# A hybrid decoder trunk on one core: one wait ahead of a table load, a weight split amid the squares, a head's sum one block later

## The chip, the cores and the metric

The kernel runs on one core of a Trainium2 chip. Times are device microseconds of one execution; the time before is the median of 3 runs.

## The reference

The reference is a trunk of two layers over 256 tokens of width 1024, batch 1, all in float32. Each layer adds to the residual stream x half of a SwiGLU block of the normed x, then a mixer, then half of another SwiGLU block:

```python
def swiglu(h, w_in, w_out):
    gate, up = jnp.split(h @ w_in, 2, axis=-1)
    return (jax.nn.silu(gate) * up) @ w_out

for i in range(DEPTH):                       # DEPTH = 2, N_A = 1
    x = x + 0.5 * swiglu(rms_norm(x, ffn1_norm[i]), ffn1_w_in[i], ffn1_w_out[i])
    hm = rms_norm(x, mix_norm[i])
    x = x + (retention(hm, ...) if i < N_A else window_attention(hm, k_sh, v_sh, ...))
    x = x + 0.5 * swiglu(rms_norm(x, ffn2_norm[i]), ffn2_w_in[i], ffn2_w_out[i])
    if i == N_A - 1:
        k_sh, v_sh = shared_kv(x, kv_norm, kv_w, k_norm)
```

The inner width of SwiGLU is 2816. Retention has 4 heads of key width 256 and value width 512, with a decay mask; its result is normed for each head, `out * rsqrt(mean(out * out) + eps) * silu(g)`, and multiplied by a matrix of 2048 x 1024. The attention of the second layer has 16 query heads, 2 key heads and a window of 128.

## The kernel before

**Numbers in two parts.** The products run on TensorE in the type fp32r. A weight tile and an activation tile are each split into a high part (`w_hi`, `h` columns 0 to 255), which ScalarE copies out, and a low part (`w_lo`, columns 256 to 511), which VectorE gets by subtraction. A block of 128 x 128 weights then takes two matmuls: high weights times both parts of the activations (512 columns), low weights times the high part (256 columns). The two halves of the result are added in the evacuation: ScalarE copies the low half out of PSUM (L365, L398), VectorE adds it to the high half (L712, L758).

**Units and slots.** All weights are laid out as 1 MB units of 2048 columns (units of the output products are somewhat smaller) and pass through four slots of `stage`, `w_hi` and `w_lo`. SyncE loads unit u when the low part of unit u - 4 is done (`lo_ready`), ScalarE's `split` (L323) waits for `landed` and, from unit 4 on, for `used`; VectorE's `split` (L641) waits for `hi_ready`; TensorE waits for `lo_ready` and increments `used`. Each engine has its own instruction stream, written out by hand in order; semaphores tie them together.

**The start.** Units 0 and 1 are loaded as eight quarters and unit 2 as two halves; ahead of each quarter a tile of x is loaded (x tile 1 and the gains from ScalarE's queue, L607 and L608, all else from SyncE's). For each of the eight tiles ScalarE makes the high part of h (L344: x times the norm's gain) and of the quarter (L613), VectorE the low parts (L687, L1090). TensorE has 9 warm-up matmuls ahead (L1581). The factor 1/rms of a token isn't needed for the products; it is applied in the evacuation (L718). So the squares of x come behind the splits of units 0 to 2: ScalarE makes four activations of two tiles each (L621), VectorE adds them up (`first_sums`, L1069), then unit 3 is split on both engines. TensorE sums over the partitions with a matmul by ones (`norm_sum`, L1177). For the first norm this stands in group 1 behind the four blocks of kt 4, which is the first quarter of unit 3, and it waits for `in_free` 3 (L1244), since it writes to a bank of group 0, and for `sum_added`. VectorE's `first_groups` (L732) begins with `add_halves_of(0)` (L712), which increments `in_free`.

**The retention's end.** GpSimd sums the squares of a head's output (L1141, L1145), TensorE sums over partitions (`head_sum`, L1356), VectorE makes the root (`norm_y`, L939), ScalarE stores the high part of y (L499) and VectorE the low part (L959, `y_lo`). The output projection has 8 tiles (d) of 16 blocks (k); the first 12 blocks of a tile need heads 0 to 2 alone. While the last head is being normed, TensorE does `early[d]` blocks of tiles 0 to 3: 12, 12, 12 and 4. The last head's sum stands behind the blocks of tile 0 (L1378). Then it waits for `y_lo` and does the other blocks, tile by tile.

Of the kernel before, what the change touches and what calls it, by code (L numbers as in the profile page):

```python
# [23 lines left out]
ALU = mybir.AluOpType  # L24
# [16 lines left out]
HEADS_R, DK, DV = 4, 256, 512  # L41
# [81 lines left out]
def trunk(nc, x_t, gains, w_in, w_out, w_ret, w_ret_out, w_kv, w_q, w_o, rot, decay, rope, head_gains,  # L123
# [29 lines left out]
    x_sq = at("x_sq", [P, DT, T], F32, aux + 8192)  # L153
# [33 lines left out]
    gain = at("gain", [P, (NORMS + 1) * DT], F32, misc + 25600)  # L187
# [10 lines left out]
    sem = nc.alloc_semaphore  # L198
# [3 lines left out]
    x_loaded = [sem(f"x_loaded{d}") for d in range(DT)]  # L202
    first_landed = [sem(f"first_landed{d}") for d in range(DT)]
    first_hi, first_lo = sem("first_hi"), sem("first_lo")
    half_landed, half_hi, half_lo = sem("half_landed"), sem("half_hi"), sem("half_lo")
    gains_loaded, rot_loaded = sem("gains_loaded"), sem("rot_loaded")
    rope_loaded, mask_loaded = sem("rope_loaded"), sem("mask_loaded")
    ones_ready, tables_ready = sem("ones_ready"), sem("tables_ready")
    x_squared = sem("x_squared")
# [56 lines left out]
    with nc.Block() as block:  # L266
# [55 lines left out]
        def _(act):  # L322
            def split(u, i=0):  # L323

                n, s = columns(u), u % SLOTS
                if not n:
                    return
                if u >= SLOTS:

                    act.wait_ge(used, u - SLOTS + 1 + 4 * i)  # L330

                act.wait_ge(landed[s], 16 * (u // SLOTS + 1) + 16 * i)
                nc.scalar.activation(w_hi[:, s, 0:n], stage[:, s, 0:n], ACT.Copy).then_inc(hi_ready, 1)  # L333

            def h_hi_tile(m, d, i=0, per=0):

                if m:

                    act.wait_ge(x_done, CREDIT + DT * (m - 1) + d + 1 + per * i)
                else:  # L340
                    act.wait_ge(x_loaded[d], 16)

                act.wait_ge(gains_loaded, 16)
                nc.scalar.activation(h[:, ds(d + per * i, 1), 0:T], x[:, ds(d + per * i, 1), :], ACT.Copy,  # L344
                                     scale=gain[:, ds(m * DT + d + per * i, 1)]).then_inc(h_hi, 1)

# [257 lines left out]
                    if d in (4, 7):  # L604
                        split(v + {4: 2, 7: 3}[d])

            act.dma_start(gain[:], gains).then_inc(gains_loaded, 16)  # L607
            act.dma_start(x[:, 1, :], x_t[1, :, :]).then_inc(x_loaded[1], 16)  # L608
            for d in range(DT):
                s, cols = quarter(d)  # L610
# [4 lines left out]
            for q in range(2):  # L615
# [2 lines left out]
                nc.scalar.activation(w_hi[:, 2, cols], stage[:, 2, cols], ACT.Copy).then_inc(  # L618
                    hi_ready if q else half_hi, 1)
            for k in range(4):  # L620
                nc.scalar.activation(x_sq[:, 2 * k:2 * k + 2, :], x[:, 2 * k:2 * k + 2, :],  # L621
                                     ACT.Square).then_inc(x_squared, 1)
            split(3)
            ffn(0)
            for c in range(HEADS_R):
                ret_head(c)
# [11 lines left out]
        def _(dve):  # L638
            chain = Chain(dve, dve_chain)

            def split(u, i=0, per=4):  # L641

                n, s = columns(u), u % SLOTS
                if not n:
                    return

                dve.wait_ge(hi_ready, u + 1 + per * i)
                nc.vector.tensor_tensor(w_lo[:, s, 0:n], stage[:, s, 0:n], w_hi[:, s, 0:n].bitcast(F32),  # L648
                                        ALU.subtract).then_inc(lo_ready, 1)
# [418 lines left out]

            def first_sums():  # L1069

                dve.wait_ge(x_squared, 4)
                half = x_sq[:, 0:4, :]
                chain.step(nc.vector.tensor_tensor(half, half, x_sq[:, 4:8, :], ALU.add))
                chain.step(nc.vector.tensor_tensor(x_sq[:, 0:2, :], x_sq[:, 0:2, :], x_sq[:, 2:4, :], ALU.add))
                nc.vector.tensor_tensor(sq_sum[:], x_sq[:, 0, :], x_sq[:, 1, :], ALU.add).then_inc(sum_added, DT)

            dve.sem_inc(in_free, CREDIT)
# [21 lines left out]
                nc.vector.tensor_tensor(w_lo[:, 2, cols], stage[:, 2, cols], w_hi[:, 2, cols].bitcast(F32),  # L1099
                                        ALU.subtract).then_inc(lo_ready if q else half_lo, 1)  # L1100
            first_sums()
            split(3)
            ffn(0)
            retention()
            ffn(1)
# [47 lines left out]
        def _(pe):  # L1153
# [202 lines left out]
            def head_sum(c):  # L1356


                pe.wait_ge(sum_added, added_for(RET) + c)
                pe.wait_ge(sum_read, sums_before(RET) + c)  # L1360
                matmul(ps[:, SUM, 0:T], ones[:], sq_sum[:], True, True).then_inc(sum_done, 1)

            def retention():
                with pe.Fori(0, 2) as i:
                    ret_head(0, i)
                    ret_head(1, i)
                u0 = FIRST["ret_out", 0]
                three = YT - YT // HEADS_R
                early = (three, three, three, 4, 0, 0, 0, 0)

                pe.wait_ge(pair_free, 4 + 4 * HEADS_R)
                pe.wait_ge(y_lo, HEADS_R - 1)
                for d in range(4):
                    pe.wait_ge(lo_ready, u0 + d + 1)
                    for k in range(early[d]):
                        weight_block(d, (u0 + d) % SLOTS, k, y_t[:, k, :], k == 0, False)
                    if d == 0:
                        head_sum(HEADS_R)  # L1378

                pe.wait_ge(y_lo, HEADS_R)  # L1380
                for d in range(DT):
                    if d >= 4:
                        pe.wait_ge(lo_ready, u0 + d + 1)
                    for k in range(early[d], YT):
                        last = weight_block(d, (u0 + d) % SLOTS, k, y_t[:, k, :], k == 0, k == YT - 1)
                    last.then_inc(used, 1)
# [272 lines left out]
```

## Time and profile before

| what | us |
|---|---|
| time, median of 3 runs | 1018.96 |
| lowest and highest run | 1018.81, 1019.04 |
| the profiled execution's own time | 1018.74 |
| its span (first to last instruction) | 1016.9 |
| TensorE busy | 1012.0 |
| VectorE busy | 779.8 |
| ScalarE busy | 496.9 |
| GpSimd busy | 95.8 |

The profile has one execution. Engines: PE is TensorE's matmuls, PEld its weight loads, DVE is VectorE, ACT is ScalarE, POOL is GpSimd, SP is SyncE; a name with q (ACTq, SPq) is that engine's queue of waits and DMA issues. L344 is line 344 of the kernel before. Matmuls overlap, so what counts of them is the distance from start to start. "idle before <- releaser" is how long an engine stood idle before a row and what ended it. The granted TensorE clock is full in every slice of the span.

### The profile page before, as it was taken

Reading aid. Unit: us, or ns where it says so; the run is one execution under the profiler, and the core shown is the slowest. Engines: PE = TensorE matmul, PEld = TensorE weight load, DVE = VectorE, ACT = ScalarE, POOL = GpSimd, SP = SyncE. Lnnn points to the kernel's source line nnn. Section 1 sums busy time; section 2 is a strip of 40 time slices with the busy share of each in tenths; the row PEclk is TensorE's granted clock in tenths of the full one; section 3 lists DMA queues with packets and bytes.
Section 4 is the critical chain, followed back from the end, with each engine's and each line's share of the span. In section 5 each row is a group of like instructions: output and inputs, shape, how many; then the busy total and the mean of one; then the engine's idle time right before and its main releaser. Section 6 shows DMA issues by size and latency. Waiting matters only on the chain.

```text
span 1016.9 us, 15833 instructions
## 1 busy us (share of the span) xinstructions
PE 1012.0 (100%) x5922; PEld 885.1 (87%) x5922; DVE 779.8 (77%) x874; ACT 496.9 (49%) x536; POOL 95.8 (9%) x91
## 2 busy tenths in 40 slices
PE   9999999999999999999999999999999999999998
PEld 8888888888888888888888888888887898888888
DVE  7988867788788687777767787787778977877743
ACT  7455445544444364455444454465447944554432
POOL 0000013101100151000014100000210041000000
PEclk9999999999999999999999999999999999999999
DMA  9664456652553454555455645545563345544461
GB/s 345 243 239 174 142 176 220 248 207 103 204 189 117 172 184 153 206 201 167 147 185 203 248 165 189 192 145 171 183 240 120 105 161 192 207 165 167 154 195 63
DMA packets 32295, 185.31 MB, mean 182 GB/s; under 512 B 3840, under 2 KB 6400, under 8 KB 16128
## 3 DMA queue, kind: packets, MB, share of 16 engines
q1 hardware_dynamic: 31968, 184.64, 51.3%
q8 instruction: 23, 0.38, 0.1%
q10 hardware_dynamic: 288, 0.16, 0.1%
q14 instruction: 16, 0.13, 0.0%
HBM read 183.73 MB, written 1.05 MB: 182 GB/s over the span
## 4 chain that ended last, share of the span: by engine, by line
PE 98%; ACT 0%; POOL 0%; DMA 0%; issue 0%; DVE 0%; POOLq 0%; ACTq 0%
PE ps L1155 98%; PE ps L1455 1%; DMA gain<-gains_dram 0%; POOL y_sq L1141 0%; PE ps L1422 0%; ACT w_hi L333 0%; ACT L344 0%; ACT y_sq L493 0%; POOL sq_sum L1145 0%; ACT gate L471 0%; ACT h L344 0%; DVE h L687 0%; PE ps L1414 0%; DVE x L813 0%; POOLq L1138 0%
## 5 line engine op out<-in xcount | busy, mean ns | idle before, releaser
L1155 PE MATMUL ps<-h,w_hi 128*128 128x512 f32 x1664 | 581.3, 395 | 0.4 <-DVE h L687 0.4
L1155 PE MATMUL ps<-h,w_lo 128*128 128x256 f32 x1664 | 462.2, 278 | 0.0
L648 DVE TENSOR_TENSOR w_lo<-stage,w_hi 128x2048 fp32r<-128x2048 f32 (+1 forms) x190 | 397.2, 2099 | 27.5 <-ACT w_hi L333 27.2
L1155 PEld LDWEIGHTS ps<-h,w_hi 128*128 128x128 f32 x1664 | 311.8, 187 | 72.2 <-issue 0.5
L333 ACT ACTIVATE w_hi<-stage 128x2048 fp32r<-128x2048 f32 (+1 forms) x190 | 326.9, 1728 | 6.6 <-PE ps L1155 6.2
L1155 PEld LDWEIGHTS ps<-h,w_lo 128*128 128x128 f32 x1664 | 313.0, 188 | 0.5
L1155 PE MATMUL ps<-act_t,w_hi 128*128 128x512 f32 (+1 forms) x726 | 244.8, 386 | 0.0
L1155 PE MATMUL ps<-act_t,w_lo 128*128 128x256 f32 x704 | 195.8, 278 | 0.0
L1155 PEld LDWEIGHTS ps<-act_t,w_hi 128*128 128x128 f32 x726 | 134.7, 188 | 29.3
L365 ACT ACTIVATE tmp<-ps 128x1024 f32<-128x1024 f32 x44 | 45.1, 1025 | 194.2 <-PE ps L1155 194.2
L1155 PEld LDWEIGHTS ps<-act_t,w_lo 128*128 128x128 f32 x704 | 132.5, 188 | 0.0
L712 DVE TENSOR_TENSOR tmp<-ps,tmp 128x1024 f32<-128x1024 f32 x44 | 53.8, 1223 | 70.0 <-ACT tmp L365 70.0
L398 ACT ACTIVATE tmp<-ps 128x256 f32<-128x256 f32 x39 | 14.9, 381 | 120.0 <-PE ps L1155 120.0
L1155 PE MATMUL ps<-w_hi,h 128*128 128x512 f32 x192 | 59.8, 393 | 0.0
L758 DVE SCALAR_TENSOR_TENSOR tmp<-ps,tmp 128x256 f32<-128x256 f32 x39 | 16.5, 422 | 54.1 <-ACT tmp L398 54.0
L370 ACT ACTIVATE tmp<-tmp 128x512 f32<-128x512 f32 x44 | 27.9, 633 | 59.1 <-DVE tmp L718 59.1
L718 DVE TENSOR_TENSOR tmp<-tmp,r_row 128x1024 f32<-128x1024 f32 x44 | 53.9, 1225 | 1.5
L1127 POOL TENSOR_TENSOR sq_sum<-sq_sum,sq 128x256 f32<-128x256 f32 x35 | 48.4, 1384 | 2.7
L1155 PE MATMUL ps<-y_t,w_hi 128*128 128x512 f32 x128 | 45.3, 399 | 0.0
L1118 POOL TENSOR_TENSOR sq_sum<-x 128x256 f32<-128x256 f32 x5 | 3.1, 615 | 443.6 <-DVE x L760 380.5
L1124 POOL TENSOR_TENSOR sq<-x 128x256 f32 x35 | 31.0, 885 | 130.8 <-DVE x L760 128.8
L1155 PEld LDWEIGHTS ps<-w_hi,h 128*128 128x128 f32 x192 | 35.4, 188 | 8.0 <-issue 0.7
(158 smaller groups left out, 737.6 us busy)
## 6 DMA issues: line engine op xcount, KB each, us to landing
stage<-w_in_dram SPq DMA_DIRECT2D x85, 1024.0 KB, 4.8
stage<-w_out_dram SPq DMA_DIRECT2D x64, 704.0 KB, 4.1
stage<-w_ret_dram SPq DMA_DIRECT2D x24, 1024.0 KB, 4.8
stage<-w_ret_out_dram SPq DMA_DIRECT2D x8, 1024.0 KB, 4.8
stage<-w_q_dram SPq DMA_DIRECT2D x4, 1024.0 KB, 5.3
stage<-w_o_dram SPq DMA_DIRECT2D x4, 1024.0 KB, 4.8
stage<-w_in_dram SPq DMA_DIRECT2D x8, 256.0 KB, 4.2
stage<-w_in_dram SPq DMA_DIRECT2D x2, 512.0 KB, 6.3
```

Source lines behind the costliest of these rows:

```text
L333: nc.scalar.activation(w_hi[:, s, 0:n], stage[:, s, 0:n], ACT.Copy).then_inc(hi_ready, 1)
L365: nc.scalar.activation(t, ps[:, 4 * (g % 2):4 * (g % 2) + 4, T:2 * T], ACT.Copy).then_inc(in_lo_half, 1)
L370: nc.scalar.activation(tmp[:, g % 2, 0:512], tmp[:, g % 2, 0:512], ACT.Silu).then_inc(in_silu, 1)
L398: nc.scalar.activation(tmp[:, d % 2, 0:T], ps[:, bank, T:2 * T], ACT.Copy, scale=scale).then_inc(out_lo_half, 1)
L648: nc.vector.tensor_tensor(w_lo[:, s, 0:n], stage[:, s, 0:n], w_hi[:, s, 0:n].bitcast(F32), ALU.subtract).then_inc(lo_ready, 1)
L712: nc.vector.tensor_tensor(t, ps[:, 4 * (g % 2):4 * (g % 2) + 4, 0:T], t, ALU.add).then_inc(in_free, 1)
L718: nc.vector.tensor_tensor(t, t, same(r_row[:], 4), ALU.mult).then_inc(in_scaled, 1)
L758: chain.step(nc.vector.scalar_tensor_tensor(t, ps[:, bank, 0:T], scale, t, ALU.mult, ALU.add))
L1124: nc.gpsimd.tensor_tensor(sq[:].rearrange("p (a n) -> p a n", a=1), x[:, ds(i + 1, 1), :], x[:, ds(i + 1, 1), :], ALU.mult).then_inc(sq_do ...
L1127: nc.gpsimd.tensor_tensor(sq_sum[:], sq_sum[:], sq[:], ALU.add).then_inc(sum_added, 1)
L1155: return nc.tensor.matmul(out_, w, x_, start=start, stop=stop)
L1455: last = nc.tensor.transpose(ps[:, P_T_BANKS[e][r], q * P:(q + 1) * P], s[:, h0 + head, kb * P:(kb + 1) * P], ident[:])
```

## The change

- The semaphore `gains_loaded` is gone. The gains' load increments `x_loaded[0]`, for which tile 0 now waits at 32 instead of 16; the second wait ahead of every h tile's activation on ScalarE (L343) is gone.
- ScalarE splits unit 3 behind the second of its four activations of squares instead of behind the fourth.
- VectorE adds the first two pairs (512 columns), splits unit 3, and then adds the other two pairs (512), both sums (512) and the two halves (256); before, it added 1024, 512 and 256 columns and then split unit 3.
- TensorE takes the last head's sum behind block 0 of tile 1 instead of behind block 11 of tile 0, and does 6 instead of 4 blocks of tile 3 ahead of the wait for `y_lo`.

```diff
--- before.py
+++ after.py
@@ -203,7 +203,7 @@
     first_landed = [sem(f"first_landed{d}") for d in range(DT)]
     first_hi, first_lo = sem("first_hi"), sem("first_lo")
     half_landed, half_hi, half_lo = sem("half_landed"), sem("half_hi"), sem("half_lo")
-    gains_loaded, rot_loaded = sem("gains_loaded"), sem("rot_loaded")
+    rot_loaded = sem("rot_loaded")
     rope_loaded, mask_loaded = sem("rope_loaded"), sem("mask_loaded")
     ones_ready, tables_ready = sem("ones_ready"), sem("tables_ready")
     x_squared = sem("x_squared")
@@ -338,9 +338,7 @@
 
                     act.wait_ge(x_done, CREDIT + DT * (m - 1) + d + 1 + per * i)
                 else:
-                    act.wait_ge(x_loaded[d], 16)
-
-                act.wait_ge(gains_loaded, 16)
+                    act.wait_ge(x_loaded[d], 16 if d else 32)
                 nc.scalar.activation(h[:, ds(d + per * i, 1), 0:T], x[:, ds(d + per * i, 1), :], ACT.Copy,
                                      scale=gain[:, ds(m * DT + d + per * i, 1)]).then_inc(h_hi, 1)
 
@@ -604,7 +602,7 @@
                     if d in (4, 7):
                         split(v + {4: 2, 7: 3}[d])
 
-            act.dma_start(gain[:], gains).then_inc(gains_loaded, 16)
+            act.dma_start(gain[:], gains).then_inc(x_loaded[0], 16)
             act.dma_start(x[:, 1, :], x_t[1, :, :]).then_inc(x_loaded[1], 16)
             for d in range(DT):
                 s, cols = quarter(d)
@@ -618,9 +616,10 @@
                 nc.scalar.activation(w_hi[:, 2, cols], stage[:, 2, cols], ACT.Copy).then_inc(
                     hi_ready if q else half_hi, 1)
             for k in range(4):
+                if k == 2:
+                    split(3)
                 nc.scalar.activation(x_sq[:, 2 * k:2 * k + 2, :], x[:, 2 * k:2 * k + 2, :],
                                      ACT.Square).then_inc(x_squared, 1)
-            split(3)
             ffn(0)
             for c in range(HEADS_R):
                 ret_head(c)
@@ -1068,10 +1067,12 @@
 
             def first_sums():
 
+                dve.wait_ge(x_squared, 2)
+                chain.step(nc.vector.tensor_tensor(x_sq[:, 0:2, :], x_sq[:, 0:2, :], x_sq[:, 2:4, :], ALU.add))
+                split(3)
                 dve.wait_ge(x_squared, 4)
-                half = x_sq[:, 0:4, :]
-                chain.step(nc.vector.tensor_tensor(half, half, x_sq[:, 4:8, :], ALU.add))
-                chain.step(nc.vector.tensor_tensor(x_sq[:, 0:2, :], x_sq[:, 0:2, :], x_sq[:, 2:4, :], ALU.add))
+                chain.step(nc.vector.tensor_tensor(x_sq[:, 4:6, :], x_sq[:, 4:6, :], x_sq[:, 6:8, :], ALU.add))
+                chain.step(nc.vector.tensor_tensor(x_sq[:, 0:2, :], x_sq[:, 0:2, :], x_sq[:, 4:6, :], ALU.add))
                 nc.vector.tensor_tensor(sq_sum[:], x_sq[:, 0, :], x_sq[:, 1, :], ALU.add).then_inc(sum_added, DT)
 
             dve.sem_inc(in_free, CREDIT)
@@ -1099,7 +1100,6 @@
                 nc.vector.tensor_tensor(w_lo[:, 2, cols], stage[:, 2, cols], w_hi[:, 2, cols].bitcast(F32),
                                         ALU.subtract).then_inc(lo_ready if q else half_lo, 1)
             first_sums()
-            split(3)
             ffn(0)
             retention()
             ffn(1)
@@ -1366,7 +1366,7 @@
                     ret_head(1, i)
                 u0 = FIRST["ret_out", 0]
                 three = YT - YT // HEADS_R
-                early = (three, three, three, 4, 0, 0, 0, 0)
+                early = (three, three, three, 6, 0, 0, 0, 0)
 
                 pe.wait_ge(pair_free, 4 + 4 * HEADS_R)
                 pe.wait_ge(y_lo, HEADS_R - 1)
@@ -1374,8 +1374,8 @@
                     pe.wait_ge(lo_ready, u0 + d + 1)
                     for k in range(early[d]):
                         weight_block(d, (u0 + d) % SLOTS, k, y_t[:, k, :], k == 0, False)
-                    if d == 0:
-                        head_sum(HEADS_R)
+                        if (d, k) == (1, 0):
+                            head_sum(HEADS_R)
 
                 pe.wait_ge(y_lo, HEADS_R)
                 for d in range(DT):
```

## Rows read from the trace of the kernel before

**Rows 1.** The page's busy table of the engines (share of the span).

```profile
PE 1012.0 (100%) x5922; PEld 885.1 (87%) x5922; DVE 779.8 (77%) x874; ACT 496.9 (49%) x536; POOL 95.8 (9%) x91
```

**Rows 2.** The chain of waits of the whole span: start us, us, what.

```profile
345.01 415.12 PE ps L1155 x2402
```

**Rows 3.** Timeline of the start: start us, us, engine, line, what, idle before.

```profile
1.19 0.45 ACTq L608 DMA_DIRECT2D x<-x_t_dram  x1
...
1.53 3.90 PE L1155 MATMUL ps<-ones 128*128 128x128 f32 x18 [1.53 <-DVE ones L1082]
...
3.34 1.28 ACT L344 ACT_TABLE_LOAD   x1 [3.34 <-DMA gain<-gains_dram]
...
4.63 0.51 ACT L344 ACTIVATE h<-x,gain 128x256 fp32r<-128x256 f32 x1
...
5.05 0.61 ACT L613 ACTIVATE w_hi<-stage 128x512 fp32r<-128x512 f32 x1
...
5.80 1.16 PE L1155 MATMUL ps<-h,w_hi 128*128 128x512 f32 x4 [0.37 <-DVE h L687]
```

**Rows 4.** Timeline of ScalarE around its other early table load.

```profile
32.10 1.28 ACT L370 ACT_TABLE_LOAD   x1
34.51 0.63 ACT L370 ACTIVATE tmp<-tmp 128x512 f32<-128x512 f32 x1 [1.13 <-DVE tmp L718]
```

**Rows 5.** DMA issues at 0.74, 1.19 and 8.78: KB, us to landing.

```profile
x<-x_t_dram SPq DMA_DIRECT2D x1, 128.0 KB, 2.3
gain<-gains_dram ACTq DMA_DIRECT2D x1, 28.0 KB, 2.5
...
stage<-w_in_dram SPq DMA_DIRECT2D x1, 256.0 KB, 3.2
...
stage<-w_in_dram SPq DMA_DIRECT2D x1, 1024.0 KB, 8.7
```

**Rows 6.** Timeline of ScalarE between unit 2 and the first copy.

```profile
15.99 2.17 ACT L621 ACTIVATE x_sq<-x 128x512 f32<-128x512 f32 x4
18.07 1.90 ACT L333 ACTIVATE w_hi<-stage 128x2048 fp32r<-128x2048 f32 x1
```

**Rows 7.** Timeline of VectorE in the same stretch.

```profile
14.84 2.51 DVE L1099 TENSOR_TENSOR w_lo<-stage,w_hi 128x1024 fp32r<-128x1024 f32 x2 [1.38 <-ACT w_hi L618]
...
19.46 0.69 DVE L1074 TENSOR_TENSOR x_sq<-x_sq 128x512 f32<-128x512 f32 x1
20.27 0.43 DVE L1075 TENSOR_TENSOR sq_sum<-x_sq 128x256 f32<-128x256 f32 x1
20.61 2.29 DVE L648 TENSOR_TENSOR w_lo<-stage,w_hi 128x2048 fp32r<-128x2048 f32 x1
22.81 1.22 DVE L712 TENSOR_TENSOR tmp<-ps,tmp 128x1024 f32<-128x1024 f32 x1
```

**Rows 8.** Waits between 14 and 30 us, then TensorE's timeline there.

```profile
PEld ps L1155 <- DVE w_lo L648: 0.3, 1, 0.3
...
24.47 0.59 PE L1155 MATMUL ps<-sq_sum,ones 128*128 128x256 f32 x2
...
25.13 0.28 PE L1155 MATMUL ps<-h,w_lo 128*128 128x256 f32 x1
```

**Rows 9.** Timeline of GpSimd and TensorE at the last head's sum.

```profile
344.22 0.74 POOL L1145 TENSOR_TENSOR sq_sum<-y_sq 128x256 f32<-128x256 f32 x1 [0.16 <-POOL y_sq L1141]
...
345.01 0.30 PEld L1155 LDWEIGHTS ps<-sq_sum,ones 128*128 128x128 f32 x2 [0.40 <-POOL sq_sum L1145]
...
345.77 0.28 PE L1155 MATMUL ps<-y_t,w_lo 128*128 128x256 f32 x1
```

**Rows 10.** Timeline of VectorE and TensorE at the output projection's start.

```profile
353.89 1.22 DVE L959 TENSOR_TENSOR y_t<-y_f,y_t 128x1024 fp32r<-128x1024 f32 x1 [1.20 <-ACT y_t L499]
...
355.26 0.41 PE L1155 MATMUL ps<-y_t,w_hi 128*128 128x512 f32 x1
...
358.84 2.29 DVE L648 TENSOR_TENSOR w_lo<-stage,w_hi 128x2048 fp32r<-128x2048 f32 x1 [3.72 <-ACT w_hi L333]
```

## The prediction

> **What bounds the kernel now.** I read the busy table first, then the chain of waits, then the timelines of the two stretches that the diff touches. The busy table gives TensorE 1012.0 us of a span of 1016.9 [rows 1]. The chain leaves TensorE for more than 0.1 us at two places before the tail only: the start, and the sum of the last retention head, from which a single piece of TensorE work of 415.12 us runs on [rows 2]. So an edit counts only as far as it moves a moment at which TensorE stands still; work on ScalarE or VectorE counts only through such a wait. The profiled execution took 1018.74 us, 1.84 us more than its span and 0.22 us less than the median of 1018.96; I sum changes in its trace and add them to the median. 0.2% is 2.0 us, about what a measurement of this kernel can tell from no change; everything below is smaller.
>
> **Part 1, one wait ahead of the first ScalarE activation.** Before, the table load starts at 3.34, when the gains have landed, takes 1.28 us, and the activation of h follows at 4.63 [rows 3]. The other table load, in front of a Silu that has one wait, runs at 32.10 at once behind the split, while its activation waits until 34.51 for VectorE [rows 4]: with one wait the load goes ahead of it. With one wait on x_loaded[0] at 32, the load should therefore follow ScalarE's second DMA issue (1.19 + 0.45 = 1.64) and end at 2.95. x tile 0 lands at 0.74 + 2.3 = 3.04, the gains at 0.74 + 2.5 = 3.24 [rows 5], so h begins near 3.3 instead of 4.63, 1.3 us earlier. The first quarter of the weight lands at 1.19 + 3.2 = 4.39 [rows 5]; its activation of 0.61 us then starts at 4.4 instead of 5.05 and ends at 5.05 instead of 5.66. TensorE, however, is in its warm-up until 1.53 + 3.90 = 5.43 and stood idle only for 0.37 us before 5.80 [rows 3]. Its gain there is bounded by 0.37 from above and 0 from below; I take 0.37, since all it needs is ready by 5.1. No DMA moves: the same transfers are issued from the same queues in the same order; only the semaphore of the gains is another. The wait taken out of every later h tile is on ScalarE, which has idle time around each of them; nothing.
>
> The Trainium skill (ScalarE: Activation LUTs, What ACT_TABLE_LOAD costs) puts a drain of about 1.38 us behind each load of 1.28 us. The trace shows the 1.28 but an activation 1.29 us after the load's start [rows 3], so no such drain here. By the rule h would begin near 4.3 and the first weight would be ready about 5.4, which is at the end of the warm-up still: the sum would be the same.
>
> **Part 2, ScalarE's and VectorE's order around unit 3.** Before, VectorE adds the squares first (1.23, 0.69 and 0.43 us) and then splits unit 3 from 20.61 to 22.90; TensorE's weight load waits 0.3 us for it [rows 7, 8]. ScalarE makes four squares from 15.99 and splits unit 3 at 18.07 for 1.90 us [rows 6].
> After: two squares, 0.52 us from start to start, end at about 17.0. Unit 3 was issued at 8.78 and lands 8.7 us later, at 17.5 [rows 5], so the split starts at about 17.5, not 17.0, and ends at 19.43. VectorE's first add (0.69) fits between 17.35, when the last half of unit 2 is done (14.84 + 2.51), and 18.0. Then it stands idle until its split S can begin at 19.47, 1.14 us earlier than 20.61. The weight is ready at 21.75; TensorE comes for it at about 22.45 (four blocks of 0.35 ahead of the sum's place, below) and no longer waits: 0.2 to 0.3 us gained. What queues behind ScalarE's wait for the landing are two squares and the copy L365.
> Behind the split there are now two adds of 512 and one of 256, where there were none. VectorE starts the next operation of another tile 2.20 us after a split's start (20.61 to 22.81), the first add costs 0.73 with its chain wait, the second 0.81 (19.46 to 20.27), the last 0.34 to the next start (20.27 to 20.61) [rows 7]. L712, which empties the banks of group 0, so starts at 19.47 + 2.20 + 0.73 + 0.81 + 0.34 = 23.55 instead of 22.81 and ends at 24.77 instead of 24.03. ScalarE's copy of the low halves (L365), which L712 needs too, follows the last two squares at about 20.4, takes 1.0 us and is in time.
> Who waits for L712: the norm's sum on TensorE, behind the four blocks of kt 4 in group 1, waits for in_free 3, which is L712. It ran at 24.47, 0.44 us after L712 [rows 7, 8], unstalled. With parts 1 and 2 TensorE comes there at 24.47 - 0.37 - 0.25 = 23.85, and must wait until 24.77 + 0.05 = 24.82. A wait of 1.0 us takes the place of both that went. Against before the sum is 0.35 us later. A stalled restart has a price as well: from the sum's start to the second matmul behind it is 0.66 us unstalled (24.47 to 25.13) and 0.76 stalled (345.01 to 345.77) [rows 8, 9], so 0.10 more. Term of the start: **+0.45 us**. Bounds: -0.6, if the wait did not bind; +0.9, if the unit landed 0.45 later. I take the value from the rows, since all durations in it are measured ones and only the landing may move.
> Next on VectorE: split 4 ends near 24.7 + 2.3 = 27.0 and the token sums at 27.4; group 2 comes for both behind 12 more blocks, at about 29.3. Split 5 (2.2), the reciprocal root (nine small steps, 4.6), a scaling of 1.2, split 6 (2.2) and the second L712 (1.2) end near 38.8; group 3 comes 32 blocks behind group 2, at 40.4. The margins are 1.9 and 1.6 us: no further wait.
>
> The Trainium skill (DMA: Bandwidth & Descriptors, Queues, rings and completion order) says that a ring's descriptors are consumed in ring order. By that rule unit 4, queued behind unit 3, can't delay its landing even when issued a little earlier, and the landing stays at 17.5. The trace does not tell, as it has only one order of issues.
>
> **Part 3, the last head's sum and two more blocks.** GpSimd's sum ends at 344.22 + 0.74 = 344.96 and TensorE's sum runs at 345.01, though the blocks of tile 0 left it free at 344.76 [rows 9]. One block later (pitch 0.35, from 345.77 to 355.26 with 27 of them [rows 9, 10]) the sum comes at 345.11, more than 0.1 us after its input: the stall of 0.25 goes and with it the 0.10 of a stalled restart. Lower bound 0, if the margin of 0.1 us fails; upper 0.4. The weights of tile 1, for which the sum now waits too, are split by then, as VectorE has no more split to do ahead of the norm.
> VectorE's chain behind the sum begins 0.1 us later, so the last low half of y, which ended at 353.89 + 1.22 = 355.11, ends at 355.21. TensorE came at the wait at 355.26 and now, with two more blocks (+0.69) and 0.35 less of stall, comes at 355.6. It does not wait; with four blocks it would have, by 0.3. The blocks are the same in number, so nothing is added. Tile 0's weights are released 0.35 us later, and unit 4 of this projection is split at 359.2 instead of 358.84 [rows 10]; TensorE comes for it at 363.2, when it has been ready for 1.7 us. Term of the retention: **-0.35 us**.
>
> **The sum.** +0.45 - 0.35 = +0.10; 1018.74 becomes 1018.84, and the median 1018.96 becomes **1019.06 us**.
>
> **The rivals.**
> Rival A, the norm's sum does not wait: L712 is early enough, because unit 3 lands before the squares are done and VectorE fits its adds in. For it: the 0.44 us that L712 had in hand. Against it: these are 0.6 less by TensorE's own gain, and VectorE has to do 0.75 us of late work. With the split at 17.0, L712 ends at 24.3, term -0.1 + 0.1; with no wait at all -0.37 - 0.25 = -0.62. With -0.35 the times are 1018.6 and 1018.0.
> Rival B, slower: unit 3 lands later than the 17.5 of before, while the DMA engines are saturated. Before, ScalarE came at 18.07 and had 0.5 us in hand; now each 0.1 us goes to VectorE, L712 and TensorE in full. With 0.5 us: 1018.96 + 0.95 - 0.35 = 1019.6. It is slower than before from a landing at 17.4 on, and clearly so (by 0.3) from 17.7. Price and place are those of the norm's sum.
> Rival C, the table load stays behind the wait. Then TensorE starts at 5.80 as before and comes at the norm's sum at 24.2, still ahead of 24.82: the same 1019.06. The time can't show it, the timeline can.
> Rival D, the retention's margin of 0.1 us does not hold, or the wait for the last low half of y comes to bind: the term is -0.1 instead of -0.35, and the time 1019.3.
>
> **How the numbers follow.** Forecast 0.65 (with C in it, 0.05), A 0.13, B 0.12, D 0.10. The forecast alone holds 1018.8 to 1019.4, with 0.1 us of spread between runs (1018.81 to 1019.04). The range reaches into A's nearer time and B's: 1018.3 to 1019.8. A gain of over 2.0 us would need more than all stalls named (0.37 + 0.3 + 0.35), a loss of over 2.0 a wait at a place where I find 1.6 us of margin or more: 0.01 and 0.02.
>
> **What would show it.** Table load near 1.7 and h near 3.3; first real matmul at 5.4 to 5.5; unit 3 split on ScalarE at 17.5; no wait for unit 3; L712 ending at 24.8 and the norm's sum right behind it, with TensorE idle for about 1 us ahead of it; the last head's sum at its place without a gap. The forecast is wrong if TensorE has no gap at the norm's sum, if the split of unit 3 starts later than 17.7, or if a new gap stands anywhere behind 25 us.

## The result and the profile after

| | before | changed |
|---|---|---|
| median of 22 runs, us | 1018.54 | 1021.22 |
| lowest, highest | 1017.78, 1019.24 | 1017.77, 1022.75 |
| the profiled execution, its span | 1018.74, 1016.9 | 1018.94, 1017.2 |

The ratio is 1.0019, 95% interval [1.0013, 1.0025]: slower by about 2 us, outside the range of 1018.3 to 1019.8. The median hides how: the 22 runs lie in two groups, 9 between 1017.77 and 1018.94 (median 1018.16) and 13 between 1021.00 and 1022.75 (median 1021.44), with none between; 3.3 us apart. The mean granted clock of each of the 22 runs is 1.00. No run of the kernel before lies in such a second group, here or in the later comparisons (90 more runs, up to 1019.47, one stray run of 1244.59 at a granted clock of 0.753 aside).

The profiled execution is one of the short group, and the longest of it. Its timeline of the start answers to [rows 3, 6, 7 and 8]; columns are start us, us, engine, line (of the changed kernel), what, idle before:

```profile
1.52 4.21 PE L1155 MATMUL ps<-ones 128*128 128x128 f32 x18 [1.52 <-DVE ones L1083]
1.68 1.28 ACT L342 ACT_TABLE_LOAD   x1 [1.68 <-PEq L1648]
...
3.09 0.51 ACT L342 ACTIVATE h<-x,gain 128x256 fp32r<-128x256 f32 x1
...
5.50 0.63 ACT L611 ACTIVATE w_hi<-stage 128x512 fp32r<-128x512 f32 x1 [1.89 <-DMA stage<-w_in_dram]
...
6.27 1.16 PE L1155 MATMUL ps<-h,w_hi 128*128 128x512 f32 x4 [0.53 <-ACT w_hi L611]
...
17.39 1.92 ACT L333 ACTIVATE w_hi<-stage 128x2048 fp32r<-128x2048 f32 x1 [0.39 <-DMA stage<-w_in_dram]
...
17.13 0.68 DVE L1071 TENSOR_TENSOR x_sq<-x_sq 128x512 f32<-128x512 f32 x1
19.41 2.29 DVE L647 TENSOR_TENSOR w_lo<-stage,w_hi 128x2048 fp32r<-128x2048 f32 x1 [1.60 <-ACT w_hi L333]
21.62 0.69 DVE L1074 TENSOR_TENSOR x_sq<-x_sq 128x512 f32<-128x512 f32 x1
22.34 0.69 DVE L1075 TENSOR_TENSOR x_sq<-x_sq 128x512 f32<-128x512 f32 x1
23.14 0.42 DVE L1076 TENSOR_TENSOR sq_sum<-x_sq 128x256 f32<-128x256 f32 x1
23.48 1.22 DVE L711 TENSOR_TENSOR tmp<-ps,tmp 128x1024 f32<-128x1024 f32 x1
...
24.75 0.70 PE L1155 MATMUL ps<-sq_sum,ones 128*128 128x256 f32 x2 [0.18 <-DVE tmp L711]
...
25.52 0.28 PE L1155 MATMUL ps<-h,w_lo 128*128 128x256 f32 x1
```

The rows show the forecast's chain nearly to the tenth: the table load at 1.68, h at 3.09, unit 3's split on ScalarE at 17.39, on VectorE at 19.41, its three late adds from 21.62 on, L711 (L712 of the kernel before) ending at 24.70, and the norm's sum at 24.75 with TensorE idle ahead of it, its weight loads for 0.50 us instead of the 1.0 of the forecast. One row is off: the first quarter landed at 5.47 instead of 4.4 (ScalarE 1.89 us idle for it), so the first real matmul is at 6.27, not 5.45. That took up half of the wait at the norm's sum; as TensorE waits there in any case, nothing of it reached the end.

The last head's sum answers to [rows 9, 10]:

```profile
344.61 0.74 POOL L1145 TENSOR_TENSOR sq_sum<-y_sq 128x256 f32<-128x256 f32 x1 [0.16 <-POOL y_sq L1141]
...
345.41 0.30 PEld L1155 LDWEIGHTS ps<-sq_sum,ones 128*128 128x128 f32 x2
...
346.18 0.28 PE L1155 MATMUL ps<-y_t,w_lo 128*128 128x256 f32 x1
...
354.29 1.23 DVE L958 TENSOR_TENSOR y_t<-y_f,y_t 128x1024 fp32r<-128x1024 f32 x1 [1.20 <-ACT y_t L497]
359.75 2.29 DVE L647 TENSOR_TENSOR w_lo<-stage,w_hi 128x2048 fp32r<-128x2048 f32 x1 [4.24 <-ACT w_hi L333]
```

GpSimd ends at 345.35, the sum's weights are loaded at 345.41 without an idle bracket, y's low half ends at 355.52, and TensorE's blocks go on around it. The time of this execution was forecast as 1018.84 and came as 1018.94. The 0.1 us between them are in the rows: the next norm's sum stands 0.39 us later than before (195.35 and 195.74) instead of 0.45, and the one behind the retention 0.21 us later (394.73 and 394.94), since the retention gave its 0.35 but lost 0.17 to a slower pace of the matmuls, of which below. So far no step fails. But the short group's median of 1018.16 lies below the range as well, and 0.38 below the 1018.54 of before: the forecast had added its +0.10 to 1018.96, the median of 3 runs that were longer than most. That the profiled execution came within 0.1 us is in part luck, and nothing in it tells of a second group.

### The profile page after: what moved, and what is told of

The parts are those of the page before. It is cut to its first block, busy times and chain, and to the rows that moved or that the text cites. A ratio compares the mean times of both kernels' runs of the same rounds, so it can differ in the third digit from the quotient of the medians.

```text
span 1017.2 us, 15787 instructions
## 1 busy us (share of the span) xinstructions
PE 1011.9 (99%) x5922; PEld 885.1 (87%) x5922; DVE 780.1 (77%) x875; ACT 496.9 (49%) x536; POOL 96.0 (9%) x91
## 4 chain that ended last, share of the span: by engine, by line
PE 97%; DMA 1%; SPq 1%; DVE 1%; ACT 0%; issue 0%; DVEq 0%
PE ps L1155 97%; DMA stage<-w_in_dram 1%; PE ps L1455 1%; SPq L289 0%; SPq L287 0%; DVE w_lo L647 0%; ACT w_hi L333 0%; PE ps L1422 0%; DVE tmp L711 0%; SPq L294 0%; DVE x_sq L1075 0%; DVE x_sq L1074 0%; PE ps L1414 0%; DVE x L812 0%; DVE sq_sum L1076 0%
## 5 line engine op out<-in xcount | busy, mean ns | idle before, releaser
L711 DVE TENSOR_TENSOR tmp<-ps,tmp 128x1024 f32<-128x1024 f32 x44 | 53.8, 1223 | 69.6 <-ACT tmp L363 69.6
```

What stands on the lines that cost most here:

```text
L711: nc.vector.tensor_tensor(t, ps[:, 4 * (g % 2):4 * (g % 2) + 4, 0:T], t, ALU.add).then_inc(in_free, 1)
```

## Where the long group's time is

Two profiles of the changed kernel by stretches, the one shown above (short group) and one of its long group (e12 below, 1020.87 us): us, then busy time and instructions (x) of PE, PEld, DVE, ACT and POOL, granted clock, DMA share, GB/s. First the short one:

```profile
60.00:160.00 100.00, 100.00 (x579) 87.46 (x578) 76.35 (x68) 45.20 (x40) 5.84 (x5) 1.00 0.52 179
400.00:500.00 100.00, 100.00 (x579) 88.19 (x578) 77.92 (x65) 47.62 (x37) 0.00 (x0) 1.00 0.49 174
```

Then the long one:

```profile
60.00:160.00 100.00, 100.00 (x567) 86.67 (x567) 75.42 (x67) 45.18 (x40) 5.84 (x5) 1.00 0.50 172
400.00:500.00 100.00, 100.00 (x579) 87.41 (x577) 79.04 (x68) 47.45 (x36) 0.00 (x0) 1.00 0.49 176
```

In both TensorE is busy for all of the stretch at a full clock (1.00, the 2.4 GHz level). But the stretch from 60 to 160 has 579 matmuls in the short run and 567 in the long one; the one from 400 to 500 has 579 in both. Single rows show the same: pairs (512 columns, then 256) of TensorE's timeline in the short one, and below them in a long one (e10, 1021.36 us):

```profile
100.17 0.39 PE L1155 MATMUL ps<-h,w_hi 128*128 128x512 f32 x1
100.40 0.27 PE L1155 MATMUL ps<-h,w_lo 128*128 128x256 f32 x1
100.52 0.40 PE L1155 MATMUL ps<-h,w_hi 128*128 128x512 f32 x1
100.75 0.28 PE L1155 MATMUL ps<-h,w_lo 128*128 128x256 f32 x1
100.87 0.39 PE L1155 MATMUL ps<-h,w_hi 128*128 128x512 f32 x1
```

```profile
99.90 0.40 PE L1155 MATMUL ps<-h,w_hi 128*128 128x512 f32 x1
100.13 0.28 PE L1155 MATMUL ps<-h,w_lo 128*128 128x256 f32 x1
100.25 0.40 PE L1155 MATMUL ps<-h,w_hi 128*128 128x512 f32 x1
100.49 0.28 PE L1155 MATMUL ps<-h,w_lo 128*128 128x256 f32 x1
100.61 0.40 PE L1155 MATMUL ps<-h,w_hi 128*128 128x512 f32 x1
100.84 0.28 PE L1155 MATMUL ps<-h,w_lo 128*128 128x256 f32 x1
100.96 0.40 PE L1155 MATMUL ps<-h,w_hi 128*128 128x512 f32 x1
```

100.17, 100.52, 100.87 in the one, steps of 0.35; 99.90, 100.25, 100.61, 100.96 in the other, 0.35 and 0.36 in turn. Over whole stretches of feed-forwards 0 and 1 and of the retention's output the trace's start times give two means and no other: 346.7 ns a pair (I call it the quick rhythm) and 353.3 ns (the slow one). The kernel before has them too: its profile is slow from 9 to 22.5 us, quick in all of feed-forward 0 behind the norm's sum, and slow again in most of the retention's output. Feed-forward 0 has some 490 pairs between the norm's sum and the last step to the retention: 490 x 6.67 ns = 3.27 us, which is the distance of the two groups. The traces have it directly: from the first norm's sum to the next it is 170.99 us in the short execution (24.75 to 195.74) and 174.26 in the long ones (24.81 to 199.07 in e10, 24.29 to 198.56 in e12, 174.27). TensorE waits no longer for it, and no view of its waits shows it.

## The experiments

Theory G: TensorE loses a stretch to the 1.2 GHz level. Theory L: a landing is late and is handed on. From e7 on, theory P: a restart of TensorE picks one of two rhythms, which then holds. Each kernel is compared with the kernel before on the same chip.

**e1, part 1 alone**

```diff
-                act.wait_ge(x_loaded[d], 16)
-
-                act.wait_ge(gains_loaded, 16)
+                act.wait_ge(x_loaded[d], 16 if d else 32)
...
-            act.dma_start(gain[:], gains).then_inc(gains_loaded, 16)
+            act.dma_start(gain[:], gains).then_inc(x_loaded[0], 16)
```

> The kernel before with part 1 alone (one wait ahead of the first activation, the gains on x_loaded[0]). The changed kernel's 22 runs lie in two groups, about 1018.1 and about 1021.5, while its profiled execution, 1018.94, shows nothing of a loss of 3 us. Theory G: in the longer runs TensorE runs a stretch at 1.2 GHz, set off by what it does in its first microseconds; then this kernel, in which the first stretch is the changed one, has runs of both groups. Theory L: in the longer runs a transfer (the first quarter or unit 3) lands late and part 2 passes it on in full; then this kernel has all runs within 1017.8 to 1019.3, as before.

1017.27 to 1019.04 in 11 runs, ratio 0.9998 [0.9989, 1.0007]. One group. TensorE still stalls for unit 3 there (its weight load for 0.2 us), and the norm's sum stands 6.99 us behind unit 3's landing (16.87 and 23.86), as it does without part 1 (17.49 and 24.47: 6.98). Part 1 alone gains nothing at the sum.

**e2, part 2 alone** (ScalarE's `split(3)` behind the second square, VectorE's behind the first add)

```diff
+                if k == 2:
+                    split(3)
...
-            split(3)
...
+                dve.wait_ge(x_squared, 2)
+                chain.step(nc.vector.tensor_tensor(x_sq[:, 0:2, :], x_sq[:, 0:2, :], x_sq[:, 2:4, :], ALU.add))
+                split(3)
...
-            split(3)
```

> The kernel before with part 2 alone (unit 3 split amid the squares). Theory L (a late landing of unit 3, handed on through VectorE and L712 to the norm's sum): runs of both groups, some about 3 us longer. Theory G with the start as the cause: one group, 1018.96 + 0.45 = 1019.4 at most; G with the new pause ahead of the norm's sum as the cause: both groups.

7 runs at 1018.14 to 1019.10 and 4 at 1021.62 to 1021.88; ratio 1.0015 [1.0005, 1.0025]. The second group comes with part 2 alone. The profile (1018.88) is of the short group, and it shows what the forecast called rival B, a unit 3 that lands later than 17.5. The split that ends the wait for the landing and the weight load of the norm's sum, here and in e12:

```profile
17.86 1.92 ACT L333 ACTIVATE w_hi<-stage 128x2048 fp32r<-128x2048 f32 x1 [0.37 <-DMA stage<-w_in_dram]
...
25.23 0.30 PEld L1157 LDWEIGHTS ps<-sq_sum,ones 128*128 128x128 f32 x2 [0.62 <-DVE tmp L713]
```

```profile
16.93 1.92 ACT L333 ACTIVATE w_hi<-stage 128x2048 fp32r<-128x2048 f32 x1 [0.38 <-DMA stage<-w_in_dram]
...
24.29 0.30 PEld L1155 LDWEIGHTS ps<-sq_sum,ones 128*128 128x128 f32 x2 [0.31 <-DVE tmp L711]
```

In the one the landing is at 17.84, in the other at 16.91, and the sum follows it. In the six profiles with part 2 and nothing else ahead of the sum (the first, e2, e4, e10, e12, e13) the sum runs 7.38 or 7.39 us behind the landing; in the five without part 2 in which TensorE stalls for unit 3 (before, e1, e3, e8, e15) 6.95 to 6.99. So part 2 puts the sum 0.42 us later, whenever the unit lands, where 0.35 were forecast; and e12, with the earliest landing of the six, is of the long group. A late landing is not what makes it long.

**e3, part 3 alone**

```diff
-                early = (three, three, three, 4, 0, 0, 0, 0)
+                early = (three, three, three, 6, 0, 0, 0, 0)
...
-                    if d == 0:
-                        head_sum(HEADS_R)
+                        if (d, k) == (1, 0):
+                            head_sum(HEADS_R)
```

> The kernel before with part 3 alone (last head's sum one block later, two more blocks). By the prediction -0.35 us: about 1018.2 to 1018.6 with the before at 1018.5 to 1019.0. Theories G and L both say one group only; if two groups stand here, the cause is in the retention.

1017.45 to 1018.67, median 1017.85 to 1018.32 of before, ratio 0.9996 [0.9987, 1.0005]: in sign and size as forecast, not clear of noise. In the profile the retention's output ran quick, where that of before ran slow from 355 to 394.5 us; that alone is some 0.7 us between executions (39 us x 6.67 / 353). It may be what spreads the runs of before too, of which there is only the one profile.

**e4, the changed kernel again**

> The changed kernel itself again, for its split into two groups and a profile that may fall into the longer one. G: in a profile of about 1021.5 the granted clock is under 1.0 in some stretch and matmuls there are twice as long. L: the clock is 1.0 and TensorE has an idle gap of about 3 us with a DMA behind it.

9 of 11 runs at 1017.61 to 1019.27, 2 at 1021.30 and 1021.70. The profile fell into the short group.

**e5, the norm's sum behind kt 5** (no pause ahead of it)

```diff
-                        if m in LATE_NORMS and g == 1 and kt == 4 and isinstance(i, int):
+                        if m in LATE_NORMS and g == 1 and kt == (5 if f == 0 else 4) and isinstance(i, int):
```

> The changed kernel with the first norm's sum behind the blocks of kt 5 instead of kt 4 (feed-forward 0 only): TensorE comes there at about 25.0 and L712 has ended at 24.7, so the pause of about 0.35 us ahead of the sum goes; VectorE's and ScalarE's order and all transfers stay. Part 2 alone had 4 of 11 runs near 1021.7, parts 1 and 3 alone none of 22. Theory G (TensorE's pause ahead of the norm's sum sets off a stretch at 1.2 GHz): no run over 1019.5, median 1017.6 to 1018.0. Theory L (the transfers or the order on VectorE and ScalarE around unit 3 lose about 3 us at another place): the long group stays, a fifth to a half of the runs near 1021.3.

2 runs at 1018.37 and 1018.77, one at 1021.71, 5 at 1023.64 to 1024.07; ratio 1.0037 [1.0024, 1.0049]. The pause ahead of the sum is gone and the long group has grown: against G as I had put it. But another pause can take its place. TensorE, no longer held up at the sum, comes to the block at 51.02 only 0.14 us behind the end of VectorE's split for it (50.88) in this profile, where the changed kernel's first profile has 0.59 us (51.05 and 51.64); in e11, the same kernel, it has to wait there.

**e6, a longer pause in the changed kernel; e7, a pause in the kernel before** (the same edit)

```diff
+                if f == 0:
+                    chain.step(nc.vector.tensor_tensor(x_sq[:, 4:8, :], x_sq[:, 4:8, :], x_sq[:, 4:8, :], ALU.add))
                 add_halves_of(0, n + 1)
```

> The changed kernel with one useless add of 1024 columns (about 1.25 us) on VectorE ahead of its first L712; TensorE's pause ahead of the norm's sum grows to about 1.5 to 2 us. G: the long group holds most or all runs, near 1022.5, its profile shows a stretch with a granted clock below 1.0; the short group, if any, near 1019.3. L: the transfers are untouched, so the shares stay as they were and both groups move by 1.25.

> The kernel before with the same useless add ahead of its first L712: L712 ends at 25.3 and TensorE, which comes at 24.5, pauses for 0.8 us, while unit 3's split and all transfers are those of before. G: a long group appears, 3 us above a short one at 1019.3. L: one group only, at 1018.3 + 0.9 = 1019.2.

e6: 1019.29, 1022.50, 1022.55, 1022.94, 1024.40 (the last at a granted clock of 0.998, all others at 1.00); ratio 1.0039 [1.0026, 1.0052]. e7: 6 runs at 1019.17 to 1020.32, 6 at 1022.06 to 1023.13; ratio 1.0021 [1.0011, 1.0030]. So a pause ahead of the norm's sum brings the long group to the kernel before, whose transfers and split of unit 3 are untouched. e7's profile (1022.06) fell into the long group, the first to do so:

```profile
60.00:160.00 100.00, 100.00 (x568) 86.68 (x567) 75.33 (x68) 45.50 (x41) 5.83 (x5) 1.00 0.49 171
400.00:500.00 100.00, 100.00 (x578) 87.43 (x578) 79.81 (x70) 47.50 (x36) 0.00 (x0) 1.00 0.50 178
```

568 matmuls instead of 579 from 60 to 160, at a clock of 1.00 and with no wait or late landing behind 26 us: theories G and L both fall, and the rhythm was found here. The runs' granted clocks spoke against G from the start: at 1.2 instead of 2.4 GHz 3.3 us are lost in a stretch of 6.6, which would make the mean granted clock of 1020 us about 0.997 (an estimate from the two levels), and all 13 long runs have 1.00.

**e8, parts 1 and 3 without part 2**

> Parts 1 and 3 without part 2. Alone they measured 0.9998 and 0.9996 of before. Both theories: one group, median about 0.7 to 0.8 us below before, 1017.5.

Missed by both theories: 1018.18, 1019.35 and 9 runs at 1020.58 to 1021.73, ratio 1.0015 [1.0006, 1.0023]. Its profile (1021.73) has the slow rhythm in feed-forward 1 instead, 395 to 581 us, though TensorE does not pause at the norm's sum ahead of it:

```profile
60.00:160.00 100.00, 100.00 (x579) 87.45 (x578) 76.22 (x68) 45.20 (x40) 5.84 (x5) 1.00 0.51 178
400.00:500.00 100.00, 100.00 (x568) 86.77 (x567) 76.57 (x63) 45.67 (x36) 0.00 (x0) 1.00 0.47 170
```

**e9, the pause two ordinary blocks ahead of the sum**

```diff
                         for o in range(4):
+                            if m == 0 and g == 1 and kt == 4 and o == 2 and isinstance(i, int):
+                                pe.wait_ge(in_free, CREDIT + GROUPS * f + 1)
+                                pe.wait_ge(sum_added, added_for(m))
```

> Found in the longer profiles: TensorE waits nowhere, its clock is full, but a pair of matmuls takes 353 ns from start to start instead of 347 over a whole stage (25 to 200 us in e7, 395 to 582 us in e8), 3.5 to 4 us in all. So theory G and theory L both fall; theory P: TensorE has two steady rhythms, and a restart picks one, which then holds for a stage. This kernel is the changed one with the wait for L712 two ordinary blocks ahead of the norm's sum, so that the pause stands ahead of an ordinary block and the sum itself follows without one, as in the kernel before. P, with the pause directly ahead of the fp32 sum as what lets in the slow rhythm: no long group, median 1018.7 (0.7 more than the short group for the two blocks now behind the pause). Rival P2: any restart behind 24 us, or none, can leave the slow rhythm: the long group stays, near 1022.

1018.31 to 1021.62, median 1019.03 (1018.7 expected), ratio 1.0009 [1.0000, 1.0017]. Two of 11 runs are above 1020.5, 1020.61 and 1021.62, and they are the only two whose granted clock is 0.998 and not 1.00; 0.002 of 1020 us are about 2 us (an estimate), so without it they too would be short. At a full clock no run is of the long group. The changed kernel itself had 8 of 11 in it on the same chip (7 of 10 in e10, and e12's one) and 23 of 44 in all (13 of 22, 2 of 11 in e4, and these), each at 1.00. The profile (1020.09) has the pause, and the sum two blocks later without one. It is slow ahead of the pause and quick behind the sum:

```profile
25.19 0.50 PE L1155 MATMUL ps<-h,w_hi 128*128 128x512 f32 x1 [1.08 <-DVE tmp L711]
...
26.00 0.59 PE L1155 MATMUL ps<-sq_sum,ones 128*128 128x256 f32 x2
```

So the place of the pause counts: directly ahead of the fp32 sum it lets the slow rhythm into about half of the runs, and two blocks ahead of it into none of 11.

**e10, e12, the changed kernel; e11, e5's kernel, for profiles**

> The changed kernel again, for a profile of its long group. P: where the run is near 1021.5, the pair takes 353 ns from about 25 to 200 us or from 395 to 582 us and TensorE's waits are those of the short profile; where it is near 1018, 347 ns in both. A long run whose stages all show 347 ns is against P.

> As e10: one more profile of the changed kernel. P: near 1021.5 with one of the two stages at 353 ns a pair, or near 1018 with both at 347 ns; in either case TensorE waits at the norm's sum alone.

> The kernel of e5 (the norm's sum behind kt 5) again, for a profile of its group at 1023.9, 5.5 us above its short one. P: the slow rhythm of the start, which nothing breaks now, goes on through feed-forward 0 (about 4 us), and some stage more of slow rhythm gives the rest (0.9 us for the retention's output, 3.5 us for feed-forward 1 would be too much).

e10: 3 runs at 1017.84 to 1018.98, 7 at 1021.22 to 1022.22; the profile, 1021.36, is quick until the norm's sum and slow behind it, to 200 us. e12 (1020.87) is slow from the start to 198. So the changed kernel's long runs are feed-forward 0 in the slow rhythm. e11 came at 1020.06: slow at the start, quick behind the norm's sum, where TensorE does not pause, and slow again from 51 us on. TensorE's timeline there, where it does nothing but ordinary blocks, with the weight load behind the gap:

```profile
49.88 0.39 PE L1155 MATMUL ps<-h,w_hi 128*128 128x512 f32 x1
...
50.22 0.39 PE L1155 MATMUL ps<-h,w_hi 128*128 128x512 f32 x1
50.45 0.28 PE L1155 MATMUL ps<-h,w_lo 128*128 128x256 f32 x1
50.79 0.19 PEld L1155 LDWEIGHTS ps<-h,w_hi 128*128 128x128 f32 x1 [0.38 <-DVE w_lo L647]
50.79 0.50 PE L1155 MATMUL ps<-h,w_hi 128*128 128x512 f32 x1
51.13 0.28 PE L1155 MATMUL ps<-h,w_lo 128*128 128x256 f32 x1
51.25 0.40 PE L1155 MATMUL ps<-h,w_hi 128*128 128x512 f32 x1
51.49 0.28 PE L1155 MATMUL ps<-h,w_lo 128*128 128x256 f32 x1
51.61 0.40 PE L1155 MATMUL ps<-h,w_hi 128*128 128x512 f32 x1
```

The pair's step is 0.35 up to 50.22, then TensorE stands still for 0.23 us, since VectorE's split of the weights ends at 50.73 only, and behind 50.79 it is slow until 198. A pause alone, with no fp32 matmul by it, can switch. So a wait can stand behind e5's long runs too, at a place beyond the last of which the forecast took the margin (40.4 us). Why five of them came at 1023.9 is not explained by the two profiles.

**e13, e14, an fp32 matmul of 2 columns ahead of each group of feed-forward 0's loop** (e13 the changed kernel, e14 the kernel before)

```diff
                 pe.wait_ge(in_free, GROUPS * f + g + 1 + 2 * i)
+                if f == 0 and not isinstance(i, int):
+                    matmul(ps[:, 4 * (g % 2), 0:2], ones[:], ones[:, 0:2], True, True)
```

> The changed kernel with a useless fp32 matmul by ones (2 columns) at the start of each of the 8 groups of feed-forward 0's loop, in a bank that the group then starts anew. Theory P (an fp32 sum or a pause picks the rhythm, which holds to the next one): the rhythm is picked eight times more, so it changes between groups of one profile, and feed-forward 0's share of 3.5 to 4 us comes in parts; the runs are spread between the two old groups instead of lying in two, each 8 times 0.2 to 0.4 us longer. If the rhythm is a state of the whole execution, picked once (rival R), the two groups stay 3 us apart and all groups of a profile have one rhythm.

> The same eight useless fp32 matmuls in the kernel before, whose feed-forward 0 was in the fast rhythm in each profile and whose runs have no long group. P: slow groups appear here too and the runs spread upwards by up to 4 us beyond the matmuls' own 2 to 3 us. R, or if what is picked hangs on the state before the matmul (fast stays fast): runs as narrow as before, 1018.4 plus 2 to 3 us, all groups at 347 ns.

e13: 1020.65 to 1022.80; e14: 1021.25 to 1023.40; ratios 1.0032 [1.0020, 1.0044] for both. The rhythm now changes from group to group. In e13 the groups' mean pair is 353.3 in those at 41 and 64, 75, 87 and 110 us, and 346.7 in those at 53 and 99; in e14 346.7 in that before 40.7, in the one at 75 and from 121 on, and 353.3 in the others. The matmuls in 10 us of four groups of e13:

```profile
53.00:63.00 10.00, 10.00 (x60) 8.73 (x59) 9.65 (x8) 5.00 (x4) 0.00 (x0) 1.00 0.74 266
64.00:74.00 10.00, 10.00 (x58) 8.69 (x58) 8.56 (x7) 5.27 (x4) 0.00 (x0) 1.00 0.59 210
99.00:109.00 10.00, 10.00 (x60) 8.74 (x59) 8.58 (x7) 4.89 (x4) 0.00 (x0) 1.00 0.41 161
110.00:120.00 10.00, 10.00 (x57) 8.66 (x57) 8.57 (x7) 5.20 (x4) 0.00 (x0) 1.00 0.39 139
```

60, 58, 60, 57. A state that the whole execution has from its start (rival R) can't do that, and e14 shows that the quick rhythm of before does not survive an fp32 matmul as such. In the kernel before, the norm's sum is such a matmul too, but it is followed by the quick rhythm each time; what differs from e14's I can't say.

**e15, parts 1 and 3 once more**

> Parts 1 and 3 without part 2 again, for a second profile: 9 of its 11 runs were 2.5 us or more longer than its shortest, and the one profile had feed-forward 1 in the slow rhythm (395 to 582 us) and feed-forward 0 in the fast one. P: again one stage in the slow rhythm if the run is near 1021, none if it is near 1018; which stage is open.

1017.54 us, among the shortest of all runs, and both feed-forwards are quick. e8's profile and this one are the same kernel, 4.2 us apart, and differ in one stage's rhythm (3.5 us) and in unit 3's landing (18.07 and 17.40, 0.67 us).

## Why the prediction was wrong

The mechanics of its two terms were right. Part 1: load and activation 1.7 and 1.5 us earlier, swallowed by the norm's wait in the changed kernel and by that for unit 3 in e1 (0.9998). Part 2: the landing at 17.36 (17.5 forecast) held ScalarE, L711 ended at 24.70 (24.77), the sum ran at 24.75 (24.82); the new wait took the place of both that went. At an equal landing the sum is 0.42 us later and the stalled restart 0.11 dearer (0.77 from the sum to the second matmul behind it instead of 0.66): 0.53 where the forecast had 0.45. Part 3: the stall went, margin 0.06 us instead of 0.1. Rivals A, C and D did not come. B's landing did in e2's profile (17.84), but its premise, that before had 0.5 us in hand against a late landing, was wrong: there ScalarE came late to unit 3 because it had waited for unit 2, whose last half lands 2.5 us ahead of it in each profile, so the sum of before moves with the landing too (16.87 and 23.86 in e1, 18.07 and 25.04 in e8). The chances of the four and of the two losses and gains beyond 2.0 us add up to 1.03.

The step that failed is the price of a restart: "A stalled restart has a price as well", taken as "0.10 more". It is read off the first two matmuls behind a stall and takes TensorE's pace behind that as given. The runs show that a pause, or an fp32 matmul, also settles at which of two rhythms the pairs run until the next such event, and that can be 490 pairs on: 0.10 us or 0.10 + 3.27 us, and the second in 23 of 44 runs of the changed kernel. Feed-forward 0's long group is absent without a pause directly ahead of the sum (before, e1, e3, e9) and comes with one of another make (e7). The long runs of e5 and e8 have the rhythm changed at other places, at a wait at 51 us and in feed-forward 1, as far as e11's and e8's profiles show. The forecast's bound, that a loss of over 2.0 us needs "a wait at a place where I find 1.6 us of margin or more", looked for waits alone; the loss, to which it gave a chance of 0.02, is in no wait.

The clue was in the trace of before. Between 8.7 and 22.5 us its pairs took 353 ns and behind the norm's sum 347 ns; the prediction has one pitch, 0.35, for both. What part 2 changes is what stands ahead of that sum. In the nine profiles in which TensorE comes to the sum without a pause (before, e1, e3, e5, e8, e9, e11, e14, e15) feed-forward 0 is quick behind it (in e11 and e14 until the next pause or fp32 matmul); in e5, e11 and e14 the pairs ahead of it are slow to the last one and there is no stall for unit 3, so there it is the sum behind which the rhythm changes. In the eight with the pause directly ahead of the sum four are quick behind it (the first, e2, e4, e6) and four slow (e7, e10, e12, e13), at pauses of the weight load of 0.50 to 1.27 us in the quick and 0.31 to 1.24 in the slow ones. The length alone doesn't tell them apart, nor does the rhythm ahead: e10 went from quick to slow, e2 from slow to quick.

What stays open: what in a restart picks the rhythm. Slow and quick came of the same kernel, so it is not its order alone; the first quarter landed at 4.29 to 5.47 us and unit 3 at 16.91 to 17.43 in the four profiles of the changed kernel, which shifts all starts behind them. That this is the link was not tried. Nor is it known why parts 1 and 3 together had feed-forward 1 in the slow rhythm in a profile, when neither had alone; there the sum has no pause ahead of it, so that a sum without one is not always followed by the quick rhythm. The last head's sum shows the same: slow behind it in 3 of 12 profiles without a pause ahead of it (the first, e5, e9) and in 1 of 5 with one (e1). That the pause ahead of the sum decides is shown for the first norm's sum alone.

No version tried beats both kernels clearly. Part 3 alone had the lowest median (1017.85 to 1018.32), with an interval that holds 1.

## What to carry to other kernels

Where TensorE never waits, look at its pitch: count the matmuls in equal stretches of two runs, and compare stages that do the same. Look at the granted clock of each run before its time is read: two runs of e9 would have passed for the long group. A pause that is removed or moved can change the pace of a whole stage behind it, and one profile tells of one of the paces only; time such a change in 10 runs or more and look at the groups, not at the median. A saving ahead of a wait for another engine is void until that engine's own queue is shorter too: here three adds behind the split undid it.

## What the runs showed of the hardware

- A pair of fp32r matmuls (512 and 256 columns, each with its own weight load) ran at 346.7 or 353.3 ns at a full granted clock, and kept that for some 490 pairs. In e11 a pause of 0.23 us changed it; in the profile of before it changes at 355.3 us, at the first block behind the wait for `y_lo`, with no pause of even a tenth of a us.
- The first quarter's landing, issued at 1.19 us, moved from 4.29 (e12) to 5.47 us (the first profile) from one execution to another; unit 3's, issued at 8.78 to 9.03, from 16.87 (e1) to 18.07 (e8).
- The table load took 1.28 us. In the kernel before the activation began as it ended (3.34 + 1.28 = 4.62, h at 4.63); with one wait ahead of both the load ran at 1.68 and h at 3.09, behind the landing of its data. The Trainium skill (ScalarE: Activation LUTs, What ACT_TABLE_LOAD costs) adds a drain of about 1.38 us to a load for every switch to another set of functions. No such drain is seen here, behind the first load or at a switch: at 855.79 in the kernel before the load of L370 begins 0.02 us behind the split ahead of it and ends at 857.07, and the activation is at 857.09. The switch takes 1.30 us where the Trainium skill has 2.66.
